# One transformer layer stream on one core: the order of gate banks, weight splits, column sums and first loads

## The reference

```
h      = rms_norm(x)
qkv, gates = h @ w_in                       # 9 blocks of 512 columns, then 3 x 1024 gate columns
y_a    = differential attention (4 heads, 2 x 64, chunk mask)
y_b    = band attention (8 heads, relative bias)
y_c    = stick-breaking attention (8 heads): sigmoid weights, reverse cumulative sums of log(1 - p)
x      = x + (sum_i sigmoid(gate_i) * (y_i @ P_i)) @ w_out
q      = rms_norm(x) @ peer_wq              # 8 heads x 2 halves x 128
top-16 of 128 keys per half, top-16 of the 16 x 16 sums, softmax g over those 16
x      = x + sum over chosen experts of g * gelu(h . u[e]) * v[e]     # 16384 experts
```

## Time and profile before

| what | value |
|---|---|
| median of 3 runs | 2279.7 us (2278.73 to 2285.3) |
| profiled execution, its own time | 2281.62 us |
| its span | 2279.9 us |
| PE busy | 2223.6 us, 98% |
| DVE, ACT, POOL busy | 68%, 52%, 11% |
| HBM read | 374.94 MB, 165 GB/s |

### The profile page before, as it was taken

How to read it: one execution, slowest core, us unless ns; L and a number is a source line. 1 busy time by engine, 2 the same in 40 slices (tenths; PEclk the granted TensorE clock), 3 DMA queues, 4 the chain that set the end, 5 groups by cost and what they waited for, 6 DMA issues and landing times.

```text
span 2279.9 us, 42254 instructions
## 1 busy us (share of the span) xinstructions
PE 2223.6 (98%) x14628; PEld 2018.3 (89%) x14628; DVE 1557.9 (68%) x2530; ACT 1175.7 (52%) x1932; POOL 252.1 (11%) x154
## 2 busy tenths in 40 slices
PE   8998999999999999999999989999999999999999
PEld 6777999999999998888877879999999999988887
DVE  5756767987776556666567568589777765566665
ACT  5744545477775433333366435454777744433333
POOL 1300006810000000000022000068100000000000
PEclk9999999999999999999999999999999999999999
DMA  6433554544445556656554335545444455556564
GB/s 227 139 130 112 180 181 148 182 142 138 138 138 161 189 184 187 197 188 199 193 185 148 111 112 185 182 143 174 148 138 138 140 165 188 187 186 196 191 195 155
DMA packets 103766, 377.27 MB, mean 165 GB/s; under 512 B 11761, under 2 KB 11761, under 8 KB 103153
## 3 DMA queue, kind: packets, MB, share of 16 engines
q1 hardware_dynamic: 102240, 370.72, 49.8%
q10 hardware_dynamic: 1424, 5.32, 0.7%
HBM read 374.94 MB, written 1.05 MB: 165 GB/s over the span
## 4 chain that ended last, share of the span: by engine, by line
PE 81%; DVE 14%; ACT 3%; issue 2%; DMA 0%; ACTq 0%; DVEq 0%; SPq 0%
PE ps L484 25%; PE ps L485 24%; PE ps L486 24%; PE ps L801 5%; DVE w_lo L1253 2%; DVE arena L1559 1%; PE ps L493 1%; DVE arena L1562 1%; DVE arena L1553 1%; DVE arena L1604 1%; DVE ps L1600 1%; DVE arena L1565 1%; DVE arena L1556 1%; ACT w_hi L925 1%; DVE arena L1608 1%
## 5 line engine op out<-in xcount | busy, mean ns | idle before, releaser
L484 PE MATMUL ps<-hT_hi,w_hi 128*128 128x256 f32 x2688 | 779.9, 290 | 20.0 <-DVE arena L1402 15.6
L1107 ACT ACTIVATE w_hi<-raw 128x1024 fp32r<-128x1024 f32 x512 | 521.0, 1054 | 513.7 <-PE ps L486 511.8
L486 PE MATMUL ps<-hT_hi,w_lo 128*128 128x256 f32 x2688 | 764.1, 284 | 0.0
L485 PE MATMUL ps<-hT_lo,w_hi 128*128 128x256 f32 x2688 | 764.1, 284 | 0.0
L1637 DVE TENSOR_TENSOR w_lo<-raw,w_hi 128x1024 fp32r<-128x1024 f32 x436 | 518.9, 1220 | 109.7 <-ACT w_hi L1107 109.7
L484 PEld LDWEIGHTS ps<-hT_hi,w_hi 128*128 128x128 f32 x2688 | 519.0, 193 | 25.0 <-DVE w_lo L1253 16.8
L485 PEld LDWEIGHTS ps<-hT_lo,w_hi 128*128 128x128 f32 x2688 | 519.5, 193 | 1.1
L486 PEld LDWEIGHTS ps<-hT_hi,w_lo 128*128 128x128 f32 x2688 | 518.8, 193 | 0.0
L484 PE MATMUL ps<-w_hi,wgt_hi 128*128 128x512 f32 x1024 | 398.9, 390 | 0.5 <-DVE wgt_lo L1696 0.5
L485 PE MATMUL ps<-w_lo,wgt_hi 128*128 128x512 f32 x1024 | 398.7, 389 | 0.0
L486 PE MATMUL ps<-w_hi,wgt_lo 128*128 128x512 f32 x1024 | 398.3, 389 | 0.0
(11 more groups left out here) (189 smaller groups left out, 2303.1 us busy)
## 6 DMA issues: line engine op xcount, KB each, us to landing
raw<-in_w_u SPq DMA_DIRECT2D x256, 512.0 KB, 3.3
raw<-in_w_v SPq DMA_DIRECT2D x256, 512.0 KB, 4.1
raw<-in_stream SPq DMA_DIRECT2D x192, 512.0 KB, 3.3
arena<-in_bias ACTq DMA_DIRECT2D x2, 1024.0 KB, 7.1
arena<-in_subk ACTq DMA_DIRECT2D x2, 1024.0 KB, 8.2
out<-x SPq DMA_DIRECT2D x4, 256.0 KB, 2.0
arena<-in_params ACTq DMA_DIRECT2D x2, 283.5 KB, 5.5
x<-in_x SPq DMA_DIRECT2D x2, 256.0 KB, 3.8
```

What stands on the lines that cost most here:

```text
L484: mm(out_, left[0], right[0], start=start, stop=False, skip_group_check=group)
L485: mm(out_, left[0], right[1], start=False, stop=False, skip_group_check=group)
L486: return mm(out_, left[1], right[0], start=False, stop=stop, skip_group_check=group)
L1107: f(w_hi[:, slot, :], raw[:, slot, :], ACT.Copy).then_inc(hi_ready.sem, 1)
```

## The change

It changes five things.

1. Gate stage: DVE does `after_gates(i - 1)` ahead of `score_max(i + 2)`, and in it copies a finished gate bank ahead of the split of the same slot. ACT copies the transposed probabilities ahead of the exponents.
2. q, k, v stage: `c_later(0)` and `c_later(1)` move one slot on, and with them the copies, exponents and masks that follow them. The second `ab_transposes` moves along.
3. `EARLY` is 20 instead of 18, and so `LATE` is 12 instead of 14; the number of early slots in the tables of GpSimd, ACT and DVE follows from it.
4. The start: SP issues all four tiles of x, two ahead of weight slot 0 and two between weight slots 0 and 1. ACT issues none. SP's program is written out for each layer.
5. Between layers: DVE makes the first split of the next layer after the second of the four additions to x.

```diff
-EARLY = 18
+EARLY = 20
@@ SP
-            for n in range(2):
-                sp.dma_start(x_tile(n), x_in[:, n, 0:512]).then_inc(x_ready[n].sem, 16)
+            def load_x(n):
+                sp.dma_start(x_tile(n), x_in[:, n % 2, (n // 2) * 512:(n // 2 + 1) * 512]).then_inc(x_ready[n].sem, 16)
...
-            with sp.Fori(0, LAYERS) as layer:
-                with sp.Fori(0, N_STREAM // SLOTS) as r:
-                    for k in range(SLOTS):
-                        load(layer, r * SLOTS + (k + 1 - SLOTS), k,
...
+            for layer in range(LAYERS):
+                def load_stream(r, k):
+                    load(layer, r * SLOTS + (k + 1 - SLOTS), k,
+                         stream[bass.ds(r * SLOTS + (layer * N_STREAM + k), 1), :, :].rearrange("a p n -> p (a n)"))
+                for k in range(SLOTS):
+                    if layer == 0 and k < 2:
+                        load_x(2 * k)
+                        load_x(2 * k + 1)
+                    load_stream(0, k)
+                with sp.Fori(1, N_STREAM // SLOTS) as r:
                     for k in range(SLOTS):
+                        load_stream(r, k)
@@ PE, table of q, k, v
-                    17: ((ab_transposes, 0),), 20: ((c_later, 0),), 21: ((c_later, 1), (ab_transposes, 1)),
+                    17: ((ab_transposes, 0),), 21: ((c_later, 0),), 22: ((c_later, 1), (ab_transposes, 1)),
@@ ACT
-            act.wait_ge(x_ready[1].sem, 16)
-            for n in range(2, 4):
-                act.dma_start(x_tile(n), x_in[:, n - 2, 512:1024]).then_inc(x_ready[n].sem, 16)
...
                 for i in range(16):
+                    if i:
+                        take_probT(i - 1)
                     if i + 1 < 16:
                         exponents_of(i + 1)
                     if i:
-                        take_probT(i - 1)
                         after_gates(i - 1)
@@ DVE
-                split((0,))
+                if layer == 0:
+                    split((0,))
...
-                        split((N_QKV + n + SLOTS,))
                         if n % 2:
                             take_gate(n // 2)
+                        split((N_QKV + n + SLOTS,))
...
                     probabilities(i)
+                    if i:
+                        after_gates(i - 1)
                     if i + 2 < 16:
                         score_max(i + 2)
-                    if i:
-                        after_gates(i - 1)
...
                     v.tensor_tensor(x_tile(n), x_tile(n), ps[:, 4 + 2 * t + half, :], ALU.add
                                     ).then_inc(x_ready[n].sem, 16)
+                    if n == 1 and layer + 1 < LAYERS:
+                        split((0,), layer + 1)
```

More of the change, by code:

```diff
@@ L351, in load @@
                 sp.dma_start(raw[:, slot, :], source).then_inc(w_loaded[slot].sem, 16)
-            with sp.Fori(0, LAYERS) as layer:
-                with sp.Fori(0, N_STREAM // SLOTS) as r:
+            for layer in range(LAYERS):
[8 more added lines that the diff above has]
+                with sp.Fori(1, N_STREAM // SLOTS) as r:
                     for k in range(SLOTS):
-                        load(layer, r * SLOTS + (k + 1 - SLOTS), k,
-                             stream[bass.ds(layer * N_STREAM + (r * SLOTS + k), 1), :, :].rearrange(
-                                 "a p n -> p (a n)"))
+                        load_stream(r, k)
                 def load_u(j, n, slot, signal=w_ready):
-                    load(layer, n, slot, w_u[bass.ds(layer * KEYS + j, 1), :, :].rearrange("a p n -> p (a n)"), signal)
+                    load(layer, n, slot, w_u[bass.ds(j + layer * KEYS, 1), :, :].rearrange("a p n -> p (a n)"), signal)
                 def load_v(j, n, slot):
@@ L1030, in _ @@
                     14: ((c_exponents, 0),), 15: ((c_exponents, 1),), 16: ((c_logs, 0),), 17: ((c_logs, 1),),
-                    18: ((take_ab_transposes, 0),), 22: ((take_ab_transposes, 1), (c_weights, 0)),
-                    23: ((c_weights, 1),), 25: ((c_weights, 2),), 26: ((c_weights, 3), (take_ab_transposes, 2)),
+                    18: ((take_ab_transposes, 0),), 23: ((c_weights, 0), (take_ab_transposes, 1)),
+                    24: ((c_weights, 1),), 25: ((c_weights, 2),), 26: ((c_weights, 3), (take_ab_transposes, 2)),
                     27: ((c_weights, 4),), 28: ((c_weights, 5),),
@@ L1248, in _, with split @@
             for layer in range(LAYERS):
-                def split(n):
+                def split(n, layer=layer):
                     for i in n:
@@ L1391, in _ @@
                     19: ((c_sums, 1), (head_norm, 3)), 20: ((c_keep, 1), (head_block, 2)),
-                    21: ((c_take_later, 0), (head_norm, 4)), 22: ((c_take_later, 1), (head_norm, 5)),
-                    24: ((c_take_later, 2), (head_block, 3), (c_mask, 0)), 25: ((c_take_later, 3), (c_mask, 1)),
-                    26: ((c_take_later, 4), (head_norm, 6)),
+                    22: ((c_take_later, 0), (head_norm, 4)), 23: ((c_take_later, 1), (head_norm, 5)),
+                    24: ((c_take_later, 2), (head_block, 3)), 25: ((c_take_later, 3), (c_mask, 0)),
+                    26: ((c_take_later, 4), (head_norm, 6), (c_mask, 1)),
                     27: ((c_take_later, 5), (head_norm, 7), (c_mask, 2)),
```

## The result

The changed kernel took 2241.5 us (median of 4, 2240.5 to 2242.3) where the kernel before took 2281.2 (median of 4, 2278.7 to 2285.3): ratio 0.9824, 95% interval [0.9807, 0.9841]. The span fell from 2279.9 to 2239.6 us, 40.3 us; the sum said 40.7.

The account below looks back on a forecast made before the run. PE bounds the kernel, busy 2223.6 of 2279.9 us; only idle and half-clock time can come back. 24.6 + 10.4 + 0 + 3.8 + 1.0 + 0.9 = 40.7 us less gives 2239.0, range 2230 to 2257 (the forecast's own 2230 to 2246).

Parts of the forecast that it names:

- the sum: Whole kernel: all predicted gains added together, 40.7 us less.
- gate stage, waits: Gate stage: PE's waits for the bank copy and, beyond the first step, for probabilities go; 24.6 us.
- gate stage, clock: Gate stage: with the waits gone PE's granted clock returns to 1.00; 10.4 us, bounds 0 and 12.
- sums one slot on: q, k, v stage: PE's wait moves to the third sum and does not go; 0, bounds +4.0 and -3.6.
- 20 early pairs: Around the routing: PE's waits for routing and POOL's w_lo go; 3.8 us, bounds 2 and 5.
- start: Program start: x tiles on SP's queue let first products begin at about 11.3; 1.0 us gained, bounds -0.5 and 2.8.
- between layers: Layer border: moving DVE's split shortens PE's 2.0 us wait for the rest of h; 0.9 us gained.
- The prediction's reason: Gate stage: the maximum comes 0.8 us late after a one-slot step and catches up in the next; PE loses 0.
- Rivals two and three: Gate stage: maximum-to-split loop bounds PE in one-slot steps, 2262, chance 0.12; or coupled in every step, 2287, chance 0.03.
- Rival one: Gate stage: the waits go but the clock still falls, as by the bank-cycling rule; 2249.4, chance 0.15.
- Rival four: Gate stage: another wait (the weights) lies right beneath, so the order does not free the banks; 2274, chance 0.04.
- The bound below zero: q, k, v stage sums: -3.6 us if a new wait of 2 us brings the clock down in both layers.

Follow-up runs that it names:

- experiments 1 to 3: Kernel before with new gate order alone, 2245.9 us; changed kernel with old gate order, 2276.4 us; kernel before with bank copy ahead of split, 2270.4 us.
- Experiment 9: Changed kernel with 18 early and 14 late pairs, as before the change; one time of 2248.1 us.
- experiment 5: Changed kernel with ACT again waiting for x tile 1 and issuing the last two x tiles; one time of 2242.1 us.
- `h_first`, experiment 6: Changed kernel with ACT rounding h ahead of weight slot 1 and loading the parameters only then; 2238.6 us.
- `both`: Changed kernel with h rounded ahead of weight slot 1 and DVE copying the first two sums earlier; 2234.1 us.
- `all_copies`: Changed kernel with h rounded ahead of weight slot 1 and DVE copying every sum a slot or more earlier; 2230.5 us.
- `bank_first`: Kernel before with only the gate bank's copy moved ahead of the split of the same slot; 2270.4 us.
- `gate_only`: Kernel before with only the gate stage's three changes of order; 2245.9 us.

## Why the prediction was right, step by step

Lengths between the marks, kernel before minus changed kernel, in one profile each; the sum of the measured column is 40.4 of 40.3 us, by rounding.

| term | predicted | measured | how |
|---|---|---|---|
| gate stage, waits | 24.6 | 24.6 | stage length less busy time |
| gate stage, clock | 10.4 | 9.7 | 0.44 of PE's busy time at a clock of 0.50 |
| gate stage, busy time beside waits | none | 2.5 | busy time, equal matmuls, less the row above |
| sums one slot on | 0 | -1.4 | layer 0: 1/rms matmul to probabilities 117.6, now 117.5; layer 1: first product to probabilities 128.8, now 130.3 |
| 20 early pairs | 3.8 | 6.2 | gate stage to layer's end, 3.1 each |
| start | 1.0 | -2.2 | 1/rms matmul at 26.9, was 24.7 |
| between layers | 0.9 | 1.0 | wait for hT_lo 2.0, now 1.0 |

**Gate waits: right**, as experiments 1 to 3 show one edit at a time. Each long wait was a copy or an end of probabilities queued behind DVE work that PE or ACT released late. The loop of maximum, exponents, rounding and split, which now has the splits in it, costs PE nothing: inside the stage PE is idle 0.1 us a layer, and its 1.6 us of waits for the maximum are those that it had before. The prediction's reason holds too. DVE's maxima at 161.87, 166.54 and 172.93 are 4.7 and 6.4 us apart, PE's scores at 161.05, 165.04 and 172.01 4.0 and 7.0: the loop falls 0.7 us behind in the one-slot step and regains 0.6 in the two-slot step. The prediction had 5.0 and 6.2 against 4.2 and 7.0. Rivals two and three are out: they would have had PE wait for the maximum in the one-slot steps.

**Clock: right, and near in size for this pair of profiles.** The windows of the earlier trace rows hold all five low stretches. Layer 0 was priced at 3.3 and is 3.0; layer 1 was priced at 7.0 and is 6.7. What the sum has at nothing is the busy time that comes with the waits at full clock, 2.5 us. The size of the clock's share is not a fixed one: the executions of the kernel before had mean granted clocks of 0.993 to 0.998. By estimate (0.44 of the time at 0.50, which is twice one minus the clock, times the span) that is 4 to 14 us in the whole run. Rival one is refuted: the waits are gone and the clock is 1.00 over both stages. The Trainium skill (TensorE: Matmul & The Clock Gate, A second HAM failure mode: psum-queue depth-cycling) ties the swings of the clock to short idles of PE between the groups of a kernel that cycles banks. Here two banks are still cycled and the idles are gone, with PE busy 87.0 of 87.1 us at full clock. That refutes the reading in rival one, by which the low stretches would stay without the waits; it does not contradict the page. Rival four is out too: nothing else lay beneath the banks' waits.

**Sums: right in mechanism.** The wait moved and did not go. The prediction had it at 2.0 us; it is 2.3. The third sum starts where it did, 68.4 us behind the 1/rms matmul in the kernel before (93.15 - 24.71) and 68.5 in the changed one (95.38 - 26.92):

```profile
95.38 0.70 PE L592 MATMUL ps<-arena 128*128 128x512 f32 x1 [2.34 <-DVE arena L1380]
```

The bound below zero was real in one layer: in layer 1 the clock falls behind the new wait. PE's third sum there, and the window:

```profile
1206.24 1.72 PE L592 MATMUL ps<-arena 128*128 128x512 f32 x2 [2.33 <-DVE arena L1380]
```

```profile
1206.00:1212.00 6.00, 5.75 (x16) 4.06 (x17) 3.31 (x5) 4.41 (x8) 4.27 (x3) 0.72 0.74 251
```

**Early pairs: the term was too small.** Both waits that were to go went (2.2 and 1.6 us). The step that failed is "PE's 2.9 us for the first one-hot rows (L801) stay": 1.3 us of them went (now L809, 1.6), and 0.2 of those for L1186 (2.3 us, now 2.1 for L1192). That makes 5.3 us of waits; the other 0.9 lies in PE's busy time in these stretches. Experiment 9 puts it back: 7.2 us in the two stretches, 0.9 of it the wait at the border that is not the pairs'. Which part of the chain behind L809 got faster was not tried.

**Start: the wrong sign.** Two sizes failed. The first is "It now stands behind half a megabyte of x, 1.4 us ... less about 0.6 for its earlier issue: 9.0", slot 1's landing: it landed at 10.9, and at 10.6 to 10.9 in all six profiles with this start and ACT's order as it is. There was no earlier issue: slot 1 was issued at 3.22, before at 3.10, since SP now issues two tiles of x ahead of it. And an earlier issue bought nothing in the one kernel that has it: in experiment 5 slot 1 was issued at 2.26 and landed at 8.7, where the three other kernels with the old start had it at 3.10 and 8.2 to 8.5. The parameters that ACT loads (284 KB) were issued at 2.47, ahead of slot 1, and are not in the estimate. In the three kernels in which they are issued at about 8 (`h_first`, `both`, `all_copies`) slot 1 lands at 9.9 to 10.1, on the mean 0.7 earlier. So of the 1.9 us between 9.0 and 10.9 0.6 is the issue and about 0.7 the parameters; the rest stays open. The second size is "more of them run at 1.2 GHz: I take 0.7 off". In the changed kernel 12 products from 13.39 on follow each other by 0.43 us, then by 0.23; in the kernel before it was 3. That costs 1.9 us. (The profile's clock column reads 1.00 over 13.39:18.68, so here the half speed is read from the pace alone.) The direction given in the prediction (ACT rounds slot 1 before h, so the weights decide) was right, and experiment 6 turns it into the gain. The 2.2 us is one pair of profiles; over ten it is about 1.1, all of it pace, since the first product came 0.25 us earlier on the mean.

**Between layers: right.** The split now stands between the second and third additions, and PE's wait is 1.03 instead of 2.04 us. Over all profiles it is 2.0 in the three kernels without the edit and 0.9 to 1.1 in the ten with it. DVE in the changed kernel, then PE:

```profile
1121.75 1.22 DVE L1259 TENSOR_TENSOR w_lo<-raw,w_hi 128x1024 fp32r<-128x1024 f32 x1
...
1123.87 0.69 DVE L1743 TENSOR_TENSOR x<-x,ps 128x512 f32<-128x512 f32 x1 [0.30 <-PE ps L494]
```

```profile
1126.60 0.50 PE L492 MATMUL ps<-w_hi,hT_hi 128*128 128x512 f32 x1 [1.03 <-DVE hT_lo L1276]
```

The fourth addition waits for PE 0.30 us, so the split ahead of it cost nothing.

The total came out at 40.3 against 40.7 partly because errors cancelled: the busy time beside waits and the early pairs gave 4.9 us more, clock, start and sums 5.3 less. That part of the agreement is luck, as is the small size of the clock's error, since what the clock costs varies by several us from one execution to the next.

## What to carry to other kernels

On an in-order engine, put the instruction that frees a buffer ahead of any that waits for the consumer of that buffer: here DVE idled 3.75 us for PE before it freed PE's bank, and PE waited 2.9 us for that. When an order is changed, ask of every moved copy what stands ahead of it now. The wait at the third sum was foreseen that way; that at the fifth was not, and only moving all copies removed both. And a bound far from the path (loads, a first rounding) becomes the path when what covered it goes, so reorder the consumer along with the loads.

## What the runs showed of the hardware

- The length of one wait does not decide whether the clock falls. The wait of 2.3 us at the third sum brought a low stretch in layer 1 in all six kernels that have it, but in layer 0 in only one of the six. From layer 1's first product to its probabilities these take 130.2 to 130.8 us, against 126.5 to 128.8 in the six others in which the clock stays at 1.00 there.
- No wait of 2 us is needed. In `bank_first` a low stretch came behind a gate wait of 1.78 us in layer 1, and another behind the 2.04 us wait at that layer's start, while the 2.04 us wait in its layer 0 brought none. In `gate_only`, whose wait at the start of layer 1 is 2.0 us, the clock is 1.00 in the whole run.
- The loss is not fixed by the waits: the same gate waits came with 4.3 and 8.0 us of busy time more in one kernel and with 6.6 and 4.1 in another, of which only 1.2 us a layer is there at a clock of 1.00 too (`bank_first`, layer 0). Taking 1.1 us off each of the waits for the bank (the longest 2.9 to 1.8) removed 8.5 of 12.2 us of busy time in one pair of profiles.
- The first products of the program ran at half the later pace. Where PE came straight from transposes (at most 0.4 us of idle) that was 3, 6, 3 and 8 matmuls with the old start and 5 to 8 with h rounded first; behind an idle of 2.6 us it was 10 to 13.
- A load of 512 KB took 7.4 to 7.7 us to land with four tiles of x, one slot and the parameters issued ahead of it, 6.7 to 6.9 without the parameters, and 5.1 to 5.4 behind two tiles of x and one slot. Issued 0.8 us earlier in that last place, it took 6.4 and landed no earlier.
